# A third gate slot in one range, gates queued ahead of down weights, and three waits moved, in a two-layer encoder trunk

## The reference

```python
for l in range(DEPTH):                                  # 2
    h = rms_norm(x, norm1_g[l])
    proj = h @ w_in[l]                                  # 1024 -> 2304
    o_a = hgrn2_mixer(...)    # 4 heads, gated recurrence in chunks of 16; rms_norm of a head, times its gate
    o_b = gqa_attention(...)  # 8 query heads, 2 kv heads, rotary positions, softmax
    o_c = s5_mixer(...)       # 16 groups, state space, then a gated linear unit
    x = x + concatenate([o_a, o_b, o_c]) @ w_out[l]
    h = rms_norm(x, norm2_g[l])
    x = x + hier_moe(h, ...)
return rms_norm(x, final_norm_g)

def hier_moe(h, w_rg, b_rg, w_re, b_re, w_gate, w_up, w_down):
    g_sel = argmax(h @ w_rg + b_rg)                     # 1 of 4 groups
    top_val, top_idx = top_k(e_logits[tok, g_sel], 2)   # 2 of its 8 experts
    gate = p_group * softmax(top_val)
    # every token goes to its two experts, each with 1024 x 512 gate and up and 512 x 1024 down weights
    y = (silu(x_e @ w_gate[e]) * (x_e @ w_up[e])) @ w_down[e]
    out = sum over both experts of gate * y
```

## Time and profile before

| | us |
|---|---|
| median of 3 runs | 1749.3 (1749.17 to 1749.81) |
| the profiled execution | 1747.39 |
| its span | 1745.3 |
| TensorE busy, all MATMUL | 1632.8 (94%) |
| VectorE busy | 647.1 (37%) |
| ScalarE busy | 418.5 (24%) |
| GpSimd busy | 298.1 (17%) |
| q1, the hardware queue that SP fills, share of 16 DMA engines | 61.5% |

### The profile page before, as it was taken

One profiled execution on the slowest core, in us unless ns is written; L12 is line 12 of the kernel. 1 busy time (PEld: TensorE's weight loads), 2 busy tenths in 40 slices (PEclk: granted clock), 3 DMA queues, 4 the chain that ended last, 5 costly groups with the idle time before them and its releaser, 6 DMA issues.

```text
span 1745.3 us, 20544 instructions
## 1 busy us (share of the span) xinstructions
PE 1632.8 (94%) x8420; PEld 860.6 (49%) x8420; DVE 647.1 (37%) x1122; ACT 418.5 (24%) x714; POOL 298.1 (17%) x374
## 2 busy tenths in 40 slices
PE   8999999979999999998799999998999999999985
PEld 4645656554444444443356556654644444444422
DVE  1796555451111111121429774565411111112115
ACT  3564541211111111110135546402011111111101
POOL 5920680000000000000269007600000000000003
PEclk9999899989999999999999898999899999999998
DMA  7000402549999999999840003035499999999996
GB/s 309 1 1 1 146 1 37 204 163 392 425 427 429 426 427 426 427 426 427 355 175 1 1 20 127 1 100 225 157 402 426 427 427 426 425 428 427 427 426 273
DMA packets 62770, 469.90 MB, mean 269 GB/s; under 512 B 18481, under 2 KB 18609, under 8 KB 36146
## 3 DMA queue, kind: packets, MB, share of 16 engines
q1 hardware_dynamic: 50626, 444.35, 61.5%
q10 hardware_dynamic: 9744, 15.80, 2.4%
q0 software_dynamic: 2304, 8.39, 1.3%
HBM read 447.54 MB, written 18.88 MB: 267 GB/s over the span
## 4 chain that ended last, share of the span: by engine, by line
PE 62%; DMA 24%; DVE 9%; ACT 3%; issue 2%; POOL 1%; ACTq 0%; POOLq 0%; DVEq 0%
DMA ring<-wu 22%; PE bank L860 18%; PE bank L546 8%; PE bank L853 8%; PE bank L681 6%; PE bank L896 6%; PE bank L620 2%; PE bank L607 2%; PE bank L587 2%; PE bank L635 2%; DMA expert_rows<-raw 1%; DVE ring L1415 1%; DVE ring L1344 1%; PE bank L517 1%; DVE ring L1413 1%
## 5 line engine op out<-in xcount | busy, mean ns | idle before, releaser
L861 PE MATMUL bank<-ring,hbuf 128*64 128x512 f32 x1024 | 456.9, 599 | 0.0
L860 PE MATMUL bank<-ring,hbuf 128*64 128x512 f32 x704 | 311.7, 596 | 25.4 <-DMA ring<-wu 23.9
L1747 DVE COPY raw<-bank 128x256 f32<-128x256 f32 x64 | 27.2, 425 | 771.9 <-PE bank L882 771.9
L853 PE MATMUL bank<-raw,hbuf 128*128 128x256 f32 x1024 | 241.8, 391 | 6.5 <-DVE raw L1689 6.5
L896 PE MATMUL bank<-ring,raw 128*64 128x512 f32 x512 | 233.4, 598 | 5.2 <-DVE raw L1747 4.1
L898 PE MATMUL bank<-ring,raw 128*64 128x512 f32 x512 | 233.4, 598 | 0.0
L853 PEld LDWEIGHTS bank<-raw,hbuf 128*128 128x128 f32 x1024 | 193.6, 194 | 36.9 <-issue 8.3
L1990 POOL DMA_INDIRECT raw<-expert_rows,dest_i x8 | 8.0, 998 | 1191.6 <-DMA expert_rows<-raw 1189.8
L546 PE MATMUL bank<-hbuf,ring 128*128 128x512 f32 x480 | 209.9, 594 | 0.8 <-ACT raw L1005 0.8
L860 PEld LDWEIGHTS bank<-ring,hbuf 128*64 128x64 f32 x704 | 94.5, 137 | 221.7 <-issue 221.7
L1235 ACT ACTIVATE raw<-bank 64x512 f32<-64x512 f32 x64 | 37.9, 591 | 454.6 <-PE bank L861 454.6
(11 more groups left out here) (346 smaller groups left out, 2015.7 us busy)
## 6 DMA issues: line engine op xcount, KB each, us to landing
ring<-wu SPq DMA_DIRECT2D x64, 2048.0 KB, 22.0
ring<-wd SPq DMA_DIRECT2D x64, 2048.0 KB, 20.2
ring<-wg SPq DMA_DIRECT2D x44, 2048.0 KB, 24.5
qd<-wg SPq DMA_DIRECT2D x20, 1024.0 KB, 20.9
ring<-w_in SPq DMA_DIRECT2D x8, 2048.0 KB, 15.8
raw<-wg SPq DMA_DIRECT2D x20, 768.0 KB, 22.2
expert_rows<-raw ACTq DMA_DIRECT2D x120, 128.0 KB, 8.2
ring<-w_out SPq DMA_DIRECT2D x4, 2048.0 KB, 7.8
```

The costliest lines, as they stand in the source:

```text
L853: last = mm(pb[n % 2][:, GC * i:GC * i + GC], h[:, b, P * k:P * k + P], pick[group % 2][:, b, :], start=(b == 0), stop=(b == NB - 1))
L860: mm(pb[2 + par][0:CAP, :], tokens[:, k, :], gates[k], start=(k == 0), stop=(k == KT - 1))
L861: last = mm(pb[2 + par][CAP:P, :], tokens[:, k, :], W_up[par][:, k, :], start=(k == 0), stop=(k == KT - 1))
```

## The change

Five edits, all in both layers:

1. `raw` and `qd` become views of one tile `raw_qd`. `slot_ids` and the overflow selections change places, so that the third gate slot is one range of 4096 columns across both, loaded in one transfer (L446).
2. In SP's order the gates of expert e+1 are issued directly behind the up weights of e, for e from 2 to 8 (`LEADING = 9`); from expert 10 on gates go ahead of their own up weights as before.
3. `turned(0)` waits for `ho_r` at 1, which now counts the second logarithm. `head_norm` waits for one more than before.
4. The tokens' positions are counted in two halves: TensorE takes `hot1` as soon as it stands, then `hot2`. `chosen` is no longer built.
5. The group logits less their maximum (L1645 before) are formed after the experts are selected.

```diff
-        raw = sb("raw", [P, 9216])
-        qd = sb("qd", [P, 2048])
+        raw_qd = sb("raw_qd", [P, 11264])
+        raw, qd = raw_qd[:, 0:9216], raw_qd[:, 9216:11264]
...
-        slot_ids = raw[:, 7168:7168 + GC]
-        pick_o, pick_ot = (raw[:, 6656 + 256 * i:6912 + 256 * i].rearrange("p (b s) -> p b s", b=NB) for i in range(2))
+        slot_ids = raw[:, 6656:6656 + GC]
+        pick_o, pick_ot = (raw[:, 7168 + 256 * i:7424 + 256 * i].rearrange("p (b s) -> p b s", b=NB) for i in range(2))
...
-        spare = [(qd[:, 0:2048], 0), (raw[:, 7424:8960], 2048), (raw[:, 6656:7168], 3584)]
-        W_spare = [area[:, at:at + 512] for area, _ in spare for at in range(0, area.shape[1], 512)]
+        spare = raw_qd[:, 7168:11264]
+        W_spare = [spare[:, 512 * k:512 * k + 512] for k in range(KT)]
...
                 if e % 3 == 2:
-                    for area, first in spare:
-                        sp.dma_start(area, here[:, first:first + area.shape[1]]).then_inc(s_spare, 16)
+                    sp.dma_start(spare, here).then_inc(s_spare, 16)
...
             for e in range(2, NE):
                 at = 3 * (e % 2)
-                gates(e)
+                if e < 3 or e > LEADING:
+                    gates(e)
                 sp.wait_ge(s["gu"], e - 1)
                 sp.dma_start(ring[:, at + 1, :], wu[layer * NE + e]).then_inc(slot[at + 1], 16)
+                if 2 <= e < LEADING:
+                    gates(e + 1)
                 if e >= 3:
                     down(e - 1)
...
                 if u == 0:
                     pe.wait_ge(s["ho_s"], on("ho_s") + 2)
-                    pe.wait_ge(s["ho_r"], on("ho_r") + 2)
+                    pe.wait_ge(s["ho_r"], on("ho_r") + 1)
...
-            pe.wait_ge(s["sel"], on("sel") + 1)
-            chosen = rt[8][:, 0:NB * NE].rearrange("p (b e) -> p b e", b=NB)
-            mm(pb[7][:, 0:P + NE], cst("before"), rt[8][:, 0:P + NE], start=True, stop=False)
...
+            for j in range(2):
+                pe.wait_ge(s["sel"], on("sel") + j + 1)
+                hot = rt[4 + j][:, 0:NB * NE].rearrange("p (b e) -> p b e", b=NB)
+                width = P if j else P + NE
+                mm(pb[7][:, 0:width], cst("before"), rt[4 + j][:, 0:width], start=(j == 0), stop=False)
+                for c in range(NB):
+                    last = mm(pb[7][:, NE * (c + 1):P + NE].rearrange("p (b e) -> p b e", e=NE), cst("ones"),
+                              hot[:, c, :][:, None, :].broadcast_to([P, NB - c, NE]),
+                              start=False, stop=(j == 1 and c == NB - 1))
...
                     ins = A(o_rs[p], M_BANK[p][:, :], ACT.Ln, bias=eps, scale=1.0 / HD)
-                link(ins)
+                ins.then_inc(s["ho_r"], 1)
+                act.wait_ge(s["ho_r"], on("ho_r") + 1)
...
-            act.wait_ge(s["sel"], on("sel") + 1)
+            act.wait_ge(s["sel"], on("sel") + 3)
...
-                dve.wait_ge(s["ho_r"], on("ho_r") + p + 1)
+                dve.wait_ge(s["ho_r"], on("ho_r") + p + 2)
...
-                link(TT(hot, per_block(ids, n), bc(first, n), ALU.is_equal))
+                return TT(hot, per_block(ids, n), bc(first, n), ALU.is_equal)
...
-            TT(g_rel, g_log, bc(col[0], EG), ALU.subtract).then_inc(s["gs"], 1)
-            first_of(g_hot, g_log, col[0], cst("group_id"), EG, col[9])
+            link(first_of(g_hot, g_log, col[0], cst("group_id"), EG, col[9]))
...
-            first_of(hot1, e_in, col[1], cst("expert_id"), NE, col[7])
+            first_of(hot1, e_in, col[1], cst("expert_id"), NE, col[7]).then_inc(s["sel"], 1)
+            dve.wait_ge(s["sel"], on("sel") + 1)
...
-            link(TT(chosen, hot1, hot2, ALU.add))
+            first_of(hot2, e_msk, col[2], cst("expert_id"), NE, col[8]).then_inc(s["sel"], 1)
             TT(small[:, 28:32], col[2], col[1], ALU.subtract).then_inc(s["sel"], 1)
+            TT(g_rel, g_log, bc(col[0], EG), ALU.subtract).then_inc(s["gs"], 1)
```

More of the change, by code:

```diff
@@ L258, in trunk @@
             ho="PE: HGRN outputs of a pair of heads", ho_s="ACT: HGRN output of a pair, its squares",
-            ho_m="PE: HGRN square sums", ho_r="ACT: HGRN rstd", o_a="DVE: o_a of a pair",
+            ho_m="PE: HGRN square sums", ho_r="ACT: HGRN logarithms of both pairs, then rstd of each", o_a="DVE: o_a of a pair",
             qk="PE: attention scores", mx="DVE: row maxima",
@@ L277, in trunk @@
             rlT="PE: router products of a block", rlT_e="ACT: those evacuated", rl="PE: router products by token", gs="DVE: group logits less maximum", gx2="ACT: group exp",
-            sel="DVE: experts selected", sx="ACT: exp of the second's difference", cnt="PE: positions and counts",
+            sel="DVE: first expert selected, second, difference of both", sx="ACT: exp of the second's difference", cnt="PE: positions and counts",
             dest="DVE: destinations, then weights and overflow blocks", oc="DVE: selection chain",
@@ L289, in trunk @@
             pt=16, pv=16, wo=16, bt=8, kp=8, xin=4, xw=4, zs=4, y5=1, yt=1, glu=2, h2t=4, rlT=4, rl=1, cnt=1,
-            ev_a=17, prep=3, h_e=4, act=3, h_s=4, sig_e=4, h_l=4, h_f=4, q_copy=8, vb=4, r_sq=5, ke_e=4,
-            kv_e=16, r_ln=5, r_rs=5, ho_s=2, ex=16, ho_r=2, pt_e=16, bt_e=4, ke=8, y5_e=1, gx=4, h2_a=4,
-            rlT_e=4, rms2=1, gx2=1, sx=1, ev_d=9, dve=123, lb=3, h_k=4, q_silu=4, h_c=4, head=4, r_y=5, hs_m=4,
+            ev_a=17, prep=3, h_e=4, act=2, h_s=4, sig_e=4, h_l=4, h_f=4, q_copy=8, vb=4, r_sq=5, ke_e=4,
+            kv_e=16, r_ln=5, r_rs=5, ho_s=2, ex=16, ho_r=3, pt_e=16, bt_e=4, ke=8, y5_e=1, gx=4, h2_a=4,
+            rlT_e=4, rms2=1, gx2=1, sx=1, ev_d=9, dve=120, lb=3, h_k=4, q_silu=4, h_c=4, head=4, r_y=5, hs_m=4,
             r_t=5, r_done=5, state=4, mx=16, pn=16, o_a=2, pn_e=16, o_b=16, ct=1, res=16, bt_v=4, xr=8, z=4,
-            kdiag=1, xs=1, y5_v=1, ge=2, z5=2, o_c=2, h2_d=4, h2=4, gs=1, sel=1, dest=2, moe=12, h=4, pool=152,
+            kdiag=1, xs=1, y5_v=1, ge=2, z5=2, o_c=2, h2_d=4, h2=4, sel=3, gs=1, dest=2, moe=12, h=4, pool=152,
             ang=2, tab=1, bc=2, rho=1)
@@ L831, in tensor_program @@
             last.then_inc(s["rl"], 1)
-            pe.wait_ge(s["sel"], on("sel") + 1)
-            chosen = rt[8][:, 0:NB * NE].rearrange("p (b e) -> p b e", b=NB)
-            mm(pb[7][:, 0:P + NE], cst("before"), rt[8][:, 0:P + NE], start=True, stop=False)
-            for c in range(NB):
-                last = mm(pb[7][:, NE * (c + 1):P + NE].rearrange("p (b e) -> p b e", e=NE), cst("ones"),
-                          chosen[:, c, :][:, None, :].broadcast_to([P, NB - c, NE]), start=False, stop=(c == NB - 1))
+            for j in range(2):
[7 more added lines that the diff above has]
+                              start=False, stop=(j == 1 and c == NB - 1))
             last.then_inc(s["cnt"], 1)
@@ L869, in gate_up @@
                     gates = W_spare
-                    pe.wait_ge(s_spare, 16 * len(spare) * (e // 3 + 1 + NE // 3 * layer))
+                    pe.wait_ge(s_spare, 16 * (e // 3 + 1 + NE // 3 * layer))
                 else:
```

7 lines of the change are left out of this document (4 added, 3 removed).

## The result

The changed kernel takes 1738.74 us, median of 6 runs (1735.38 to 1743.75), the one before 1749.22 (1748.44 to 1749.81, 6 runs beside them). The ratio is 0.9944, 95% interval 0.9931 to 0.9956: 10.5 us faster, where 14.6 were forecast. In a second series the same changed kernel gave 1736.77 against 1748.10, ratio 0.9932 (0.9919 to 0.9945). The profiled execution is the fastest of the first series, 1735.38 us with a span of 1733.5.

The account below looks back on a forecast made before the run. It took the weight stream to bound the expert stage and TensorE the stage ahead; 3.0 + 0.3 + 2.5 + 1.5 = 7.3 us a layer, 14.6 for two, gave 1734.7 us, range 1729.5 to 1741.

Parts of the forecast that it names:

- Head of attention: Attention loop: unit 0's transposes run beside the exponentials, unit 1's start earlier; 3.0 us a layer, 1.7 if the clock falls.
- who is late next?: S5 transposes: TensorE arrives 3 us earlier, POOL's part ends at 250.5, so 10 us of cover remain.
- Router chain: Expert selection: one VectorE operation goes and the count is split in two; 0.3 us a layer, between 0 and 0.4.
- Early gates: Expert stage: gates queued ahead of down weights fill the stream's pause near 404 us; 2.5 us a layer, bounds 1.5 to 2.7.
- the swap at experts 3 to 7 moves no byte of the sum: Expert stage: after the first pause the queue only grows, so the same swap at later downs adds nothing.
- One transfer: Third-slot gate loads: 144 packets instead of 432, nine loads in the saturated stream; 1.5 us a layer, bounds 0 to 2.5.
- The term that stood against it, 0: Third-slot loads: HBM memory's share, some 358 GB/s, binds and not the engines; term 0, sum 3.0 us smaller.
- Rival 1: Pick matmuls keep the 2.4 GHz clock: 2.1 us a layer more gained, 1730.5 us; chance 15%.
- Rival 2: Attention head does not pay, another release holds the second transposes: 6.0 us less gain, 1740.7; chance 10%.
- Rivals 3, 4 and 5: Stream not the end's bound, 1742.7, 6%; change ineffective, 1749, 3%; down weights too late, up to 1794, 3%.

Follow-up runs that it names:

- head_alone: Kernel before with only the third edit (transposes of unit 0 wait for the logarithms, not the exponentials): 1745.78 us, ratio 0.9991.
- no_head: Changed kernel with the old head of attention (TensorE waits for both exponentials again): 1740.50 us, ratio 0.9952.
- rho_act: Changed kernel with POOL's last copy and memset of the S5 part moved to ScalarE: 1732.80 us, ratio 0.9915.
- bt_act: Changed kernel with all eight B copies on ScalarE and TensorE needing VectorE's product only at the fifth kernel product: 1732.12 us, ratio 0.9903.
- lead4: Changed kernel with early gates for expert 4 alone (LEADING 4 instead of 9): 1743.30 us, ratio 0.9962.
- bt_lead4: Kernel with ScalarE's eight B copies, with early gates for expert 4 alone (LEADING 4 instead of 9): 1736.19 us, ratio 0.9933.
- router_alone: Changed kernel with the first three edits taken back, leaving the two router edits: 1747.84 us, ratio 0.9998.
- the repeat: Changed kernel run again in the second series with nothing changed: 1736.77 us, ratio 0.9932.

## Why the prediction was right, and where it was not

The direction and the range held (1729.5 to 1741.0), and what bounds the kernel was read rightly. The gain is 10.5 us where 14.6 were forecast, and 1738.74 lies at the upper edge of the forecast's own bounds, 1731 to 1739. That the range took in the shortfall is in part luck: the lower bound of the head's term, 1.7 us a layer, was set for a clock that falls, and what came instead, 1.3 to 1.85, had another cause. By the prediction's own steps, for two layers:

- **Head of attention, forecast 6.0 us, arrived 2.6 to 3.7** (`head_alone`, `no_head`). This is the term that was mis-sized. On the spot it gave 2.87 us in layer 1, within the bounds. What failed is the answer to "who is late next?". I checked POOL's part against TensorE's transposes, found 10 us of cover, and stopped there. VectorE's products for the same stage were not looked at, though they overlap POOL's instructions and showed 2.84 and 4.24 us where 2.54 is the time alone (`rho_act`). The real cover was VectorE's chain, and it was under 2 us: of 2.87 us TensorE lost 1.10 to the new wait. `bt_act` and `rho_act` took the obstacle away by different engines and gave 16.0 and 15.5 us under before, next to the 14.6 of the forecast; the other terms did not come as forecast either, so this is no proof of the sum.
- **Router chain, forecast 0.6, measured 0.6**, not told from nothing; by the landmarks the stretch from S5 products to picks is 0.4 us shorter in each layer. TensorE ran the first half of the count beside VectorE's search, at 353.83, and the second from 356.09.
- **Early gates, forecast 5.0, measured 6.1** by the medians (interval 3.5 to 7.9), but 3.5 by the landmarks of its profile (1.9 and 1.6). The pause went where it was said. One sentence of that step was false: that the swap at experts 3 to 7 moves no byte of the sum. With the first swap alone the pause comes back one expert later and costs 1.75 to 2.0 us a layer (`lead4`, `bt_lead4`).
- **One transfer, forecast 3.0, measured 2.0** by the median (interval 0 to 3.3), and 2.4 by the landmarks (1.0 and 1.4). The term that stood against it, 0, fell: with 2,550 packets fewer the same queue moves more bytes in the same time. By the median the size was half as large again as what came.
- By the landmarks gates and transfer together bring 4.3 and 3.9 us, but alone 1.9 + 1.0 and 1.6 + 1.4. What the last 1.4 and 0.9 us are stays open. In the 18 us from 412.11 the kernel with early gates alone moves 415 GB/s on average, and the changed one from 409.91, the same place of its stage, 426; that is 0.5 us.
- **The rivals.** Rival 1, picks at full clock, did not come in layer 1: they take 16.45 us, granted clock 0.50 from 361 to 365. In layer 2 they take 15.77 instead of 16.74. That is not shown to be the router's doing: `router_alone` has 16.92 and 16.93, and `head_alone`, without the router's edits, 16.58 and 15.46. Rival 2 said that the head is held in its own loop; it was not held there, but 65 us later, and not entirely. Rivals 3, 4 and 5 fell: the stage shortened, the parts did what the text says, and TensorE waited for no down weights.
- **Unforeseen:** in layer 1 the clock falls on gate-up of expert 30, the last one ahead of the last stores, where in the kernel before it fell on expert 29 (granted 0.57 from 812 to 816), with the next up weights still on their way. Windows of the profile after, TensorE alone: us, busy, clock, DMA share, GB/s.

```profile
816.00:820.00 4.00, 0.78 (x4) 1.00 1.01 430
820.00:824.00 4.00, 3.58 (x10) 0.57 1.01 425
```

Four matmul pairs take 0.8 to 1.0 us instead of 0.4, behind a wait of 3.64 us. On expert 29, behind a wait of 3.65 us, the clock had stayed at 1.00. The slow pairs are the 1.7 us by which the lead shrinks from 6.4 at 820 us to 4.7 at the stores.

## What to carry to other kernels

Where work is pulled forward, the cover must be asked of every engine that feeds the next stage, and a VectorE or POOL row whose time is longer than its kind takes elsewhere may be a sign that two engines exclude each other there. Its end is then set by the other engine, and starting it earlier gains nothing. A transfer queue that is filled once at a known pause may show the pause again one step later, so the lead has to be kept for more than one transfer. Here a lead up to expert 4 was too short and one up to expert 9 was enough; nothing between was tried. The best version found keeps the change and takes VectorE out of the S5 transposes (`bt_act`): 1732.12 us, ratio 0.9903 to the kernel before.

## What the hardware showed that I had not expected

- A VectorE product with both inputs in SBUF and a POOL sum or copy do not overlap at all: in layer 1 of thirteen of the fourteen profiles the first product ended 2.41 to 2.43 us after the POOL sum that it met, whether it had been started 0.2 or 4.9 us before that end. In the fourteenth (`no_head`) it started behind the sum, 0.3 us into POOL's copy, and ended 2.41 us after the copy, which then took 1.88 us. They take turns, instruction by instruction.
- A wait of TensorE can cost more than its length. In the S5 part nothing more was lost behind waits of 0.76 to 1.88 us (`head_alone`, after, the repeat's layer 2); behind 2.03 to 2.20 us (`lead4`, the repeat's layer 1) the clock stood at the 1.2 GHz level for a while and 1.6 to 1.7 us more went, behind 4.12 us 2.4 and behind 3.26 us 2.9. The length alone does not decide: in the expert stage after the change a wait of 3.65 us left the clock at 1.00 and the next one, of 3.64 us, did not.
- With the same bytes to move and the 16 DMA engines 96% busy with this queue in both, 11,250 packets instead of 13,800 let the stream of one core move 428 GB/s instead of 427, for nearly 400 us without a break.
